# One layer of a hybrid decoder on one core: the sample's loads in 512 KB pieces, another order on ScalarE, one last norm, and x reloaded from SyncE's queue

## What is computed

```python
h = x + W_out [ HGRN2(hn) || chunk-gMLP(hn) ],  hn = RMSNorm(x)
h = h + CrossAttn(RMSNorm(h), memory K/V)      # 4 heads, 256 memory tokens
h = h + W_down relu(W_up RMSNorm(h))^2         # 1024 -> 4096 -> 1024
y = RMSNorm_final(h)
```

## Time and profile before

| | us |
|---|---|
| median of 3 runs | 2925.42 (2924.47 to 2929.04) |
| the profiled execution, its own time | 2927.06 |
| its span in the profile | 2925.2 |
| PE busy | 2776.0 |
| POOL, ACT, DVE busy | 1061.6, 1066.7, 1603.5 |
| mean granted clock of PE | 0.977 |

### The profile page before, as it was taken

The page is one execution under the profiler, slowest core; times in us unless marked ns, Lnnn a source line. Parts: engine busy times, 40 slices in busy tenths (PEclk is TensorE's granted clock), DMA queues, the critical chain, the costliest instruction groups (busy, mean ns, idle before and its releaser), DMA issues.

```text
span 2925.2 us, 40029 instructions
## 1 busy us (share of the span) xinstructions
PE 2776.0 (95%) x16475; PEld 2214.3 (76%) x16475; DVE 1603.5 (55%) x2050; ACT 1066.7 (36%) x1379; POOL 1061.6 (36%) x682
## 2 busy tenths in 40 slices
PE   8999999999999999999878999989999999979997
PEld 7787788888888888888656777677777777757785
DVE  5578444564449353743444575445555565655555
ACT  4435223332234123422334433444443322443334
POOL 0184302212221222200334454544455554545563
PEclk9999999999999999999899999999999999989999
DMA  8895667667874778665655667556566666566542
GB/s 308 312 316 199 238 221 290 249 218 282 315 289 177 272 288 333 224 214 181 246 212 184 210 222 256 177 214 221 209 232 237 215 224 228 221 212 245 185 149 99
DMA packets 215951, 681.66 MB, mean 233 GB/s; under 512 B 22560, under 2 KB 27936, under 8 KB 198368
## 3 DMA queue, kind: packets, MB, share of 16 engines
q1 hardware_dynamic: 186576, 546.84, 53.0%
q10 hardware_dynamic: 29200, 132.33, 11.9%
HBM read 531.83 MB, written 147.26 MB: 232 GB/s over the span
## 4 chain that ended last, share of the span: by engine, by line
PE 45%; issue 28%; POOL 17%; DVE 6%; DMA 1%; ACT 1%; SPq 1%; POOLq 0%; ACTq 0%; DVEq 0%
PE half L1143 30%; POOL w_ring L1086 17%; PE half L1432 10%; PE half L1151 2%; PE half L1285 1%; DVE lvl L2665 1%; DVE lvl L2678 1%; PE half L1160 1%; PE half L1360 1%; PE half L1489 0%; DMA mem_raw<-in_w_ck 0%; DMA w_in_raw<-in_w_down 0%; SPq L725 0%; DVE stats L2768 0%; DMA w_pairs<-stage 0%
## 5 line engine op out<-in xcount | busy, mean ns | idle before, releaser
L1086 POOL TENSOR_TENSOR w_ring<-w_raw,w_ring 128x512 fp32r<-128x512 f32 x448 | 756.2, 1711 | 853.0 <-ACT w_ring L2048 852.9
L1143 PE MATMUL half<-w_ring,a_hi 128*128 128x512 f32 x2176 | 687.9, 397 | 0.0
L1432 PE MATMUL half<-pair_hi,w_ring 128*128 128x512 f32 x1792 | 587.5, 406 | 38.1 <-issue 13.6
L1432 PE MATMUL half<-w_ring,pair_hi 128*128 128x512 f32 x1760 | 558.5, 399 | 0.0
L1143 PEld LDWEIGHTS half<-w_ring,a_hi 128*128 128x128 f32 x2176 | 411.3, 189 | 97.8
L1432 PEld LDWEIGHTS half<-pair_hi,w_ring 128*128 128x128 f32 x1792 | 345.4, 193 | 133.9 <-issue 28.2
L1143 PE MATMUL half<-w_ring,a_lo 128*128 128x512 f32 x1088 | 437.5, 402 | 4.6 <-DVE a_lo L2260 3.6
L2048 ACT CAST w_ring<-w_raw 128x1024 fp32r<-128x1024 f32 x224 | 234.2, 1048 | 472.4 <-PE half L1432 141.2
L1432 PEld LDWEIGHTS half<-w_ring,pair_hi 128*128 128x128 f32 x1760 | 334.0, 190 | 80.6
L1432 PE MATMUL half<-w_ring,pair_lo 128*128 128x512 f32 x880 | 353.1, 401 | 25.6 <-DVE pair_lo L2939 19.7
L1432 PE MATMUL half<-pair_lo,w_ring 128*128 128x512 f32 x896 | 359.7, 401 | 0.0
(11 more groups left out here) (334 smaller groups left out, 3529.5 us busy)
## 6 DMA issues: line engine op xcount, KB each, us to landing
w_ring<-w_pairs SPq DMA_DIRECT2D x320, 512.0 KB, 4.2
w_raw<-w_sums SPq DMA_DIRECT2D x256, 256.0 KB, 3.3
w_pairs<-w_ring SPq DMA_DIRECT2D x64, 512.0 KB, 5.2
w_sums<-w_comb SPq DMA_DIRECT2D x32, 1024.0 KB, 6.6
ht_h<-quad ACTq DMA_DIRECT2D x32, 1024.0 KB, 5.4
raws<-ht_h ACTq DMA_DIRECT2D x32, 1024.0 KB, 6.0
raws<-xt_h ACTq DMA_DIRECT2D x28, 1024.0 KB, 6.7
w_raw<-in_w_up SPq DMA_DIRECT2D x96, 256.0 KB, 4.7
```

The lines of the kernel that those rows point to most:

```text
L1086: nc.gpsimd.tensor_tensor(w_lo[:, k, :], w_raw[:, k % RAW, :], w_hi[:, k, :].bitcast(F32), ALU.subtract).then_inc(w_split.sem, 1)
L1143: m = nc.tensor.matmul(ps[:, j, :], l, r, start=(i == 0 and q == 0), stop=(i == tiles_in - 1 and q == 2))
L1432: m = nc.tensor.matmul(ps[:, j, :], l, r, start=(i in FRESH and k == 0 and q == 0), stop=(k == KQ - 1 and q == 2), skip_group_check=i not ...
```

## The change

- SP no longer issues a sample step's loads at once. `sample_piece` issues one piece of at most 512 KB behind each weight tile of two products, the third and the fourth after the step (8 pieces for a product's weights, half a request's keys or values as one piece). The same bytes are loaded, and the waits ahead of them stay, now ahead of piece 0.
- "zqf" is loaded in this way too, at products 3 and 4, and the tiles of product 0 are issued ahead of the `raws`.
- On ACT `up_out` comes first in products with a sample step; the square and the store of product 6 of a group (`up_squared`) come behind the rounding for the next product. In `slot(0)` the operand of product 2 is rounded ahead of the scaling of x.
- The scaling and the stores at the turn from `down0` to `down1` move one place later on ACT (behind the rounding for products 85 and 86), and SP begins the reloads of x, behind the first tile of products 86 (quad 0), 87 (quads 2 and 1) and 88 (quad 3).
- The last norm is done once for the four row groups, without `last_gained`; quad 0 is scaled and gained by DVE (`y_finished`); the output goes in one transfer of 1 MB and four of 512 KB from SP, one of 1 MB from ACT.

```diff
+SAMPLE_LOADS = {0: ("first", 0), **SAMPLE_AT}
...
                 for n in range(SLOTS):
-                    g, i = divmod(n, NQ)
                     for k in range(KQ):
-                        t = n * KQ + k
-                        s = t % RAW
-                        sp.wait_ge(w_split.sem, w_split.at(pos, t) - RAW)
-                        sp.dma_start(w_raw[:, s, :], big_tile(a, g, i, k)).then_inc(w_in[s].sem, 16)
-                        if k == 1 and a * SLOTS + n - 3 in SAMPLE_AT:
-                            key = SAMPLE_AT[a * SLOTS + n - 3]
-                            sample_loads(*key)
...
+                        if a or n:
+                            load_tile(a, n, k)
+                        if a == 3 and k == 0:
+                            for q in {2: (0,), 3: (2, 1), 4: (3,)}.get(n, ()):
+                                sp.wait_ge(y_out[q].sem, y_out[q].at("down0", 0))
+                                sp.dma_start(quads[q][:], x_rows_of(1, q, x_rows_h)).then_inc(xq_in[q].sem, 16)
+                        for back in (3, 4):
+                            key = SAMPLE_LOADS.get(a * SLOTS + n - back)
+                            if key:
+                                sample_piece(*key, (back - 3) * KQ + k)
...
-                for i in range(2):
-                    sp.dma_start(w_s[i][:], I[w][0][row + 512 * i:row + 512 * i + 512, col:col + D].rearrange(
-                        "(k p) c -> p k c", p=P)).then_inc(w_s_in[i], 16)
...
+                sp.dma_start(w_s[k // 4][:, k % 4, :], I[w][0][row + P * k:row + P * k + P, col:col + D]
+                             ).then_inc(w_s_in[k // 4], 16)
...
+            for k in range(KQ):
+                load_tile(0, 0, k)
             sp.wait_ge(*done("last", ("sc", 1)))
...
-            load_product("zqf")
...
-                if ph == 2:
-                    act.wait_ge(*in_big(h_out[q], 2 * GU - 1, GU))
-                    act.wait_ge(x_out.sem, x_out.at("last", 0))
-                else:
-                    act.wait_ge(y_out[q].sem, y_out[q].at("down0", 0))
...
-                if l < 3 and ph == 3:
-                    for q in {0: (0, 2), 1: (1, 3)}.get(l, ()):
-                        x_loaded(3, q)
-                if m < TOTAL:
+                first = n in SAMPLE_AT
+                if up and first:
+                    up_out(e)
+                if m < TOTAL and n != 1:
                     weights_high(m, 0)
...
+                    weights_high(2, 0)
+                    operand_high(2)
                     n3_scaled("last")
...
+                if up and e % NQ == 6:
+                    up_squared(e)
...
                     if l == 27:
                         rsqrt(pos, "ya", TT)
-                        y_stored(ph, "ya", (0, 2))
                 if n == 3 * SLOTS:
+                    y_stored(2, "ya", (0, 2))
                     y_squared(2, 3)
                     rsqrt("down0", "yb", TT)
+                if n == 3 * SLOTS + 1:
                     y_stored(2, "yb", (1, 3))
...
+            def y_finished(q, tag):
...
+                for t in range(TT):
+                    ins = nc.vector.scalar_tensor_tensor(quads[q][:, t, :], quads[q][:, t, :], rstd[:, c + t:c + t + 1],
+                                                         gain[:, b * 512:b * 512 + 512], ALU.mult, ALU.mult)
```

More of the change, by code:

```diff
@@ new lines, in sample_piece @@
+                        if i == 0:
+                            sp.wait_ge(*step(("zqf", "zig")[e - 1]))
+                        load_product(("zig", "zuv")[e - 1], i)
+                    if e == 3 and i < 4:
+                        sp.wait_ge(*step("zuv"))
+                        sp.dma_start(s0[:, 2 * i:2 * i + 2], I["state_hgrn"][0, 2 * i:2 * i + 2].rearrange("b h k v -> k b h v")
+                                     ).then_inc(s0_in, 16)
+                    if e == 6:
+                        if i == 0:
+                            sp.wait_ge(s_out_done, 16)
+                            sp.wait_ge(*step("st1"))
+                        load_product("wo", i)
+                        if i == 7:
+                            sp.wait_ge(*step("vn"))
+                            sp.dma_start(xs[:], I["x_sample"].rearrange("b t d -> (b t) d")).then_inc(xs_in, 16)
+                            load_gain_s("g_cross")
@@ new lines, in sample_piece @@
+                if pos == "second":
+                    if e == 1:
+                        if i == 0:
+                            sp.wait_ge(*step("wo"))
+                        load_product("cq", i)
+                    if 2 <= e <= 5 and i < 4:
+                        if i == 0:
+                            sp.wait_ge(*step("cq" if e == 2 else f"kt{2 * e - 5}"))
+                        load_kv("k", 2 * e - 4 + i // 2, i % 2)
+                    if e == 6 and i < 4:
+                        if i == 0:
+                            sp.wait_ge(*step(f"kt{DB - 1}"))
+                        load_kv("v", i // 2, i % 2)
+                    if e == 7:
+                        if i < 2:
+                            sp.wait_ge(*step("pt"))
+                            load_kv("v", 2, i)
+                        if i == 7:
+                            sp.wait_ge(*step("xn2"))
+                            load_gain_s("g_mlp")
@@ L997, in sample_loads @@
+                if pos == "third":
+                    if e in (1, 2) and i < 2 * len(V_GROUPS[e]):
+                        if i == 0:
+                            sp.wait_ge(*step(f"pv{e - 1}"))
+                        load_kv("v", V_GROUPS[e][i // 2], i % 2)
+                    if e == 3:
+                        if i == 0:
+                            sp.wait_ge(*step("pv2"))
+                        load_product("co", i)
                     if 4 <= e:
-                        sp.wait_ge(*step("co" if e == 4 else f"up{e - 5}"))
@@ L1004, in _ @@
+                    load_product(f"dn{e - 1}", i)
             block_loads("first", 0, False)
@@ L2086, in up_out, with up_squared @@
                                      ).then_inc(evacuated_of(pos, job), 1)
-                if i == 6:
-                    act.wait_ge(*out(pos, job))
-                    nc.scalar.activation(quads[q][:], quads[q][:], ACT.Square).then_inc(act_sem, 1)
-                    act.wait_ge(act_sem, link.next())
-                    h_stored(e)
+            def up_squared(e):
+                q = CHAIN[e % NQ]
+                act.wait_ge(*product_out(e))
+                nc.scalar.activation(quads[q][:], quads[q][:], ACT.Square).then_inc(act_sem, 1)
+                act.wait_ge(act_sem, link.next())
+                h_stored(e)
             def h_stored(e):
@@ L2191, in slot @@
                 if m < TOTAL and m % NQ not in (1, 3):
-                    operand_high(m)
+                    if n != 1:
+                        operand_high(m)
                     weights_high(m, 1)
-                if up:
+                if up and not first:
                     up_out(e)
```

163 lines of the change are left out of this document (66 added, 97 removed).

## The result

The changed kernel takes 2874.65 us (median of 4 runs, 2871.56 to 2876.96) against 2927.23 for the kernel before (4 runs): a ratio of 0.982, 95% interval 0.980 to 0.984. It is faster by 53 us, a little over half of the 92.5 that were forecast, and outside the range. The profiled execution has a span of 2874.5 us against 2925.2, so 50.7 us went.

The account below looks back on a forecast made before the run. PE, busy 95% of the span, was taken as the bound, leaving its idle time and lost clock to win; nine terms summed to 92.5 us, from 2927.06 to 2834.6, forecast 2833 us, range 2806 to 2866.

Parts of the forecast that it names:

- Terms 2 to 7: Gains at products 7 to 10 (24 us), 14 (7), 21 to 24 (8.5), 28 and 29 (10), 35 and 42 (7), 56 to 59 (4.5).
- Term 5: Products 28 and 29: a late tile behind the step's loads and nothing else; gain 10 us.
- Term 7: Products 56 to 59: 49.86 us against 44.8 undisturbed; gain 4.5 us.
- Term 2: Products 7 to 10: the copy out of PSUM no longer waits behind late tiles; gain 24 us, 3.5 stay.
- Term 6: Products 35 and 42: no late load but a 10 us chain on ACT and DVE; gain 7 of 15.9 us.
- Term 9: Behind the last matmul: one chain of small operations instead of two, output landing at 2918.8; gain 6.5 us.
- New waits: Rival: late pieces at 7, 70, 77, 91, 98 (30 us), no gain at the turn (9 us), or both; chance 0.20.
- The slower rival: At the 14 weight loads, tile and piece served one after another, 7.5 us a pair, about 3360 us; chance 0.04.
- point 1: Sign: ACT's wait at the first tile of product 0 and at product 7 below 2 us; products 28 and 29 at 22.4.
- Point 2: Sign: gaps at 7, 35 and 42 named by ACT's copy or DVE's rest, 2 to 3 us, not by a transfer.
- Point 3: Sign: at products 86 and 87 ACT waits for tiles of `w_raw`, 4 to 6 us.
- Point 4: Sign: no product from 60 on longer than before; gaps at 70, 77, 91 or 98 ending on `w_s` or `kv` mean late pieces.

Follow-up runs that it names:

- e2: Changed kernel with ACT's order undone (copy, square and store where they were before), the pieces kept: 2881.36 us, ratio 0.984.
- e7: Changed kernel with ACT instead of SP beginning the reloads of x at the turn to `down1`: 2868.90 us, ratio 0.979.
- e11: Changed kernel with ACT's own transfers between `raws`, `ht_h` and the quads moving half of their bytes: 2856.83 us, ratio 0.974.
- e15: Changed kernel with ACT beginning x reloads and issuing pieces of steps from product 4 on, and decays moved behind the roundings of product 7: 2867.48 us, ratio 0.979.

## Why the prediction was wrong

The direction, the places and three of the nine terms were right: the start (14.3 for 16), the turn (9.7 for 9) and the end (4.8 for 6.5). At the turn even the parts came as worked out: gaps of 4.4 and 5.4 us, for about 4 and 5.6, the first with ACT waiting 4.10 us for a tile behind the reload of quad 0. The step at 42 left 2.83 of idle for 2.7.

**The step that failed** is one sentence under the terms: "in the 22.4 us of two products go 8 tiles (2.1 MB), 8 pieces (4.2 MB) and about 2.4 MB of ACT's reloads and stores, 388 GB/s" and, two sentences on, "So it fits, barely." 2.4 MB is ACT's share of an average pair of products. Its eight transfers of a group are not spread evenly: in products 5 and 6, behind the steps at product 4 of a group, there are four of them, 4.19 MB in the row of queue 10. The demand was 469 GB/s in products 5 and 6 and in 26 and 27, above the 416 that the same passage took for the limit, and 375 where a step loads 2.1 MB. The trace of the kernel before had this row too, in its view of the DMA queues over the same two products:

```profile
q10 hardware_dynamic: 556, 4.12, 48.2%
```

In the down phases, where ACT stores nothing, the same pieces fit: while PE was in products 68 and 69, the same two places of a group, 6.51 MB moved, 1.05 of them ACT's, the tiles landed after 5.3 us in the median, and no product from 60 to 83 changed its length. (SP's first tile also went out ahead of product 68 there, at 2314.99 against 2316.95.) The other number in the sentence, 22.4 us, was too large as well: in the up phases SP's part of the stream began up to 6.7 us into the two products. No run separates the two.

The terms that took a late tile as cured failed with it. Terms 2 to 7 were to bring 61 us and brought 26, or 22 with the 4.2 lost at products 16 and 18. Halving ACT's transfers brought PE's last matmul forward by 20.8 us (2840.3, against 2861.1), and 19.5 of that at products 14, 21 to 24, 28 and 29, 35 and 56 to 59. That is the measured size of what ACT's bytes cost there. It is not the whole gap of those terms, and product 7 has no part in it.

- *Term 5, product 28:* "a late tile behind the step's loads and nothing else", gain 10. Right on the cause before, wrong in that the cure was whole: 0.8. The bulk load's loss was traded for one of the same size.
- *Term 7, products 56 to 59:* gain 4.5, measured -2.9. Spreading moved the bytes out of a quiet stretch into the one in which ACT reloads x. With the old bulk load they take 46.7. This is the one place where pieces are worse than no pieces.
- *Term 2:* the copy's chain was counted from a rounding at 1512; it came 5.8 us later against PE, with the tiles. Forecast 3.5 us to stay, 10.5 did. No edit took these away: halving ACT's transfers left a gap of 7.5 us, halving the pieces left the stretch within 1 us, and moving the chain put a late piece in its place. How they divide between tile and chain stays open.
- *Term 6:* only the 2.7 of the chain was counted at 35; the tiles were late too (6.56 idle; 2.82 with ACT's transfers halved). That a stretch scatters by 1.2 to 1.4 us at 35 and 42 makes the 3.2 for 7 a rough figure.
- *Product 18* lost 3.0 us with the idle time unchanged (2.61 and 2.69), by a granted clock of 0.82. In other kernels of the study (e2, e7 and e11, products 18 to 20 in 39.3 us, as before) it did not, and no run shows why.
- *Term 9, the end:* the chain was right, the transfers were not. The four issues begin 5.9 us behind the last matmul and the fourth 7.8 behind it, as forecast (2914.8 against 2907.0), but 2 MB issued within 2 us share the engines: the last landed 5.1 us after its issue, for 4, and the span ends 0.5 us later.

**The rivals.** The time, 2874.65, lies in the stretch of "New waits" (2850 to 2880, given 0.20), and its evidence, "388 of 416 GB/s", was the right place to worry. Its mechanism was not what happened: it had piece 7 late at 7, 70, 77, 91 and 98 and the turn without gain. No piece was late outside product 7, and there only once the decays had moved. What was late were tiles, at places that the rival did not name. The range stopped at 2866 because the demand was computed from a mean; with 375 to 469 GB/s, and less than 22.4 us to move them in, the whole of terms 3 to 5 and 7 would have been in doubt, 30 us. The slower rival (each transfer served alone) is out: transfers of both queues were under way together, and 7.84 MB went in 22.4 us. On the Trainium skill's advice of 1 MiB ("DMA: Bandwidth & Descriptors", section "Bandwidth"): with 512 KB pieces, 256 KB tiles and ACT's 1 MB transfers mixed, windows of 6 and 7 us reached 412 and 404 GB/s at a DMA share above 1.00, so smaller transfers did not cost rate here; the rate of one transfer by itself is measured by no run.

Of what the profile would show, point 1 failed (5.94 us of wait ahead of product 7, 31.84 at 28 and 29; only the tiles of product 0 were no longer waited for). Point 2 held at 42; the gap at 7 is named by ACT's copy, but 7.8 long, and the one at 35 is 6.6. Point 3 held in kind, with ACT's waits for tiles of 4.10 and 8.78 us, for 4 to 6. Point 4 held but for product 87, which took 12.7 us for 11.2. Point 5 failed: 13.4 us for 11 to 12.

## What to carry to other kernels

When a bulk transfer is cut up and spread, sum the bytes of all queues in each window into which the pieces go, not over the period: a stream that fits on average was 20% above that average in two products of seven here. Ask also when the stream can start, and which engine holds it back. A loader with few places turns a landing time into a rate: four places of 256 KB carried PE where tiles landed in 6.2 us or less in the median (products 40 and 41, 68 and 69), and fell behind at 7.8 to 8.2. And before a wait is called cured, name the next one and its time; at product 7 a tile, a chain of small operations and a piece end within a few microseconds of each other, and taking one away moved nothing.

## What the runs showed of the hardware

- Moving the pieces from SP's queue to ACT's left the tiles' landing at 8.0 us (7.8 before), though nothing stood ahead of them in their own queue but tiles. An emptier queue was no fast lane while the DMA engines were full (a share of 0.96 and 1.00 from 1769 to 1786.4 in that run).
- Both queues together moved 404 and 412 GB/s over 7 and 6 us, with transfers of 256 KB, 512 KB and 1 MB under way (e15). With as much under way a 256 KB tile took 6.3 to 10.1 us to land, 8.2 in the median; the median over the kernel before was 3.3.
- The same idle time does not always cost clock. Product 14 had idle stretches of 2.61 and 1.69 us at a granted clock of 1.00, product 18 one of 2.69 at 0.82. The microsecond or two per gap that the forecast added is no rule.
